# Meta tokens moved behind the tokens in the moving operand of a two-block forward pass

## The chip, the cores and the metric

The kernel runs on one core of one Trainium2 chip. The metric is the device time of one execution in microseconds (us), as the median of the runs. TensorE (PE) does the matmuls, VectorE (DVE) and ScalarE (ACT) prepare operands and take results, GpSimd (POOL) only clears a few constants, and SyncE (SP) issues the weight DMAs.

## The reference

256 tokens of width 2048 pass through two blocks, in float32. The first has an mLSTM branch and a convolution branch, then a feed-forward part; its output is normalised. The second puts 16 meta tokens ahead of the 256 and computes, in short:

```python
h = jnp.concatenate([meta, x], axis=1)            # 16 + 256 rows
u = rmsnorm_2(h, norm1_g)
proj = u @ w_in
v_pool, v_lru, v_gelu, g_pool, g_lru = jnp.split(proj, IN_SPLITS, axis=-1)
pool_out = pool_mixer(v_pool, pool_w, pool_scale)
xc = causal_depthwise_conv(v_lru, conv_w, conv_b)
lru_out = rg_lru(xc, ...) * jax.nn.gelu(v_gelu)
merged = jax.nn.sigmoid(g_pool) * pool_out + jax.nn.sigmoid(g_lru) * lru_out
h = h + merged @ w_out
h = h + jnp.square(jax.nn.relu(rmsnorm_2(h, norm2_g) @ mlp_w1)) @ mlp_w2
out = rmsnorm_2(h, final_g)[:, 16:]
```

Only `v_pool` and `v_lru` are needed for all 272 rows, and so are the gates of the recurrence, which are computed from `xc`. Everything else is needed for the 256 tokens alone.

## The kernel before

**Numbers in two parts.** Each float32 operand is split into a high part (rounded to fp32r) and a low part (the difference). Each product is three matmuls into the same PSUM tile: high weights by high operand, high weights by low operand, low weights by high operand. Weights come in chunks by DMA into `raw`; ACT makes `whi` (line 881) and DVE makes `wlo` (line 1322), half a chunk at a time, three halves ahead of PE (`AHEAD`). There are four slots for each. Weights are the stationary operand; the features stand on the partitions, and the tokens stream.

**Phases and groups.** The program is a list of phases (`plan`), each one weight matrix or a part of it. A group is 4 output tiles of 128 features; with 16 k-tiles it has 192 matmuls of 256 columns (`group`, lines 558 to 560). PE works through two groups' PSUM in turn (`s` is 0 or 1). All engines go through the phases in the same written order. The post-processing of a group (its `step`, in parts j = 0 to 7) is spread over the splits of the group that follows: part j = 0 reads PSUM, and j = 2 of a residual phase sums squares and makes the low operand. The engines wait for each other by semaphores: PE waits for `lo_ready` ahead of every half chunk, for `psum_freed` ahead of every group, and at a phase's first group for the operand (`waits`).

**The normalised operand.** `hn` holds for each k-tile one row of 64 + 2 x 256 floats in each partition, 2304 bytes: 32 unused floats, 16 low and 16 high parts of the meta tokens, 256 high parts, 256 low parts. So the high parts of meta and tokens are one run of 272 floats from float 48 on. The low parts are not one run, and a second tensor `lo2` of 16 rows of 272 floats (1088 bytes) holds them. The gain of the norm is applied in the operand; the scale of each token (one over the root) is applied to the result on its way out of PSUM, with `scale` of 272 floats, whose first 16 are 1.0.

**Wide groups.** `pool_in` and `lru_in` (8 groups) run in `group_wide`, lines 585 to 587, 272 columns: 1536 matmuls. The gates of the recurrence (`gates`, lines 805 to 807) are 192 more, with an operand made in `xc_parts`. `copy_wide` (line 1735) takes the wide results out of PSUM.

**The step that makes the operand of the wide groups.** `down_2` is the last phase of the first block: 4 groups of 11 k-tiles, 132 matmuls each. The DVE step of each group at j = 2 is two sums of squares (line 1350, since two norms are taken together), then `low_operand(..., wide=True)`: four instructions into `hn`, and the same four again into `lo2` (line 1360).

**Halved matmuls.** In some groups one matmul of 256 columns is written as two of 128 (lines 555 and 556): at the last half chunk of a group that has operand waits, and in some phases at an early half chunk. `group_wide` has none.

**Order of tensors in a partition.** `raw`, `whi`, `wlo` and `h` are multiples of 256 bytes each; then comes `gap_a` of 192 bytes, then `hn` (16 x 2304 bytes), then `act` (16 x 2048 bytes). So, counted from the start of `whi` and modulo 256, `hn` and `act` begin at 192.

## Time and profile before

| what | value |
|---|---|
| median of 3 runs | 2707.1 us (2702.05 to 2714.29) |
| the profiled execution, its own time | 2707.32 us |
| its span in the trace | 2705.5 us |
| PE busy in the span | 2669.5 us, 99% |
| DVE busy | 1700.7 us, 63% |
| ACT busy | 1294.6 us, 48% |
| mean granted TensorE clock | 0.996 |

The span goes from the first to the last instruction; the execution's time is 1.8 us more. Matmuls are pipelined: one takes some 277 ns from start to end, and the next starts long before that. So a stretch of PE work is to be read by how many matmuls it starts, which the windows of the trace count, and not by its busy time.

### The profile page before, as it was taken

To read this page: it belongs to the slowest core of one execution; us is meant where nothing else is said; L and a number is where in the kernel's file an instruction comes from. 1 tells how busy PE (TensorE), PEld (TensorE's weight loads), DVE (VectorE), ACT (ScalarE), POOL (GpSimd) and SP (SyncE) were. 2 spreads that over 40 slices of the span, in tenths; PEclk is the share of its full clock that TensorE was granted. 3 is DMA by queue.
4 is the path that set the end of the run, shared out by engine and by line. 5 is a ranking of instruction groups with operands and counts; after the bars stand their busy time and mean duration, and the time that the engine had idled before them with its cause. 6 is when DMAs were issued, how large, how long until landed. Compare 5 with 4: busy or idle time off the path is not lost.

```text
span 2705.5 us, 53096 instructions
## 1 busy us (share of the span) xinstructions
PE 2669.5 (99%) x23022; PEld 2653.9 (98%) x23022; DVE 1700.7 (63%) x1724; ACT 1294.6 (48%) x1459; POOL 1.8 (0%) x14
## 2 busy tenths in 40 slices
PE   8999999999999999999989999999999999999998
PEld 7999999999999999999989999999999999999998
DVE  5665654566776567656785687676666555565565
ACT  6444544445554355435553456664444344343443
POOL 0000000000000000000000000000000000000000
PEclk9999999999999999999999999999999999999999
DMA  6546565555556555565445555555566565555653
GB/s 214 168 159 199 173 202 186 187 195 195 187 186 200 190 192 188 195 198 172 164 168 172 173 176 192 192 188 194 188 194 196 194 191 198 187 192 197 192 194 113
DMA packets 257822, 503.31 MB, mean 186 GB/s; under 512 B 10150, under 2 KB 19038, under 8 KB 257630
## 3 DMA queue, kind: packets, MB, share of 16 engines
q1 hardware_dynamic: 255364, 500.50, 56.1%
q8 instruction: 136, 2.23, 0.3%
q10 hardware_dynamic: 2282, 0.26, 0.1%
q14 instruction: 40, 0.33, 0.0%
HBM read 498.63 MB, written 2.10 MB: 185 GB/s over the span
## 4 chain that ended last, share of the span: by engine, by line
PE 93%; DVE 4%; ACT 2%; issue 1%; DMA 0%; SPq 0%; DVEq 0%; ACTq 0%
PE psum L559 28%; PE psum L558 28%; PE psum L560 28%; PE psum L585 2%; PE psum L586 2%; PE psum L587 2%; DVE wlo L1322 1%; ACT whi L881 1%; DVE work L1350 1%; DVE work L1678 0%; DMA work<-in_x 0%; PE psum L805 0%; PE psum L807 0%; PE psum L806 0%; PE psum L643 0%
## 5 line engine op out<-in xcount | busy, mean ns | idle before, releaser
L1322 DVE TENSOR_TENSOR wlo<-raw,whi 128x1024 fp32r<-128x1024 f32 x952 | 1159.8, 1223 | 923.3 <-ACT whi L881 920.6
L881 ACT ACTIVATE whi<-raw 128x1024 fp32r<-128x1024 f32 x952 | 1004.2, 1059 | 1229.3 <-PE psum L560 1115.6
L559 PE MATMUL psum<-hn,whi 128*128 128x256 f32 x4448 | 1233.3, 277 | 0.0
L558 PE MATMUL psum<-hn,whi 128*128 128x256 f32 x4432 | 1230.6, 278 | 1.8 <-DVE wlo L1322 1.8
L560 PE MATMUL psum<-hn,wlo 128*128 128x256 f32 x4448 | 1232.4, 277 | 0.0
L558 PEld LDWEIGHTS psum<-hn,whi 128*128 128x128 f32 x4432 | 835.5, 189 | 4.6 <-DVE wlo L1322 2.6
L559 PEld LDWEIGHTS psum<-hn,whi 128*128 128x128 f32 x4448 | 836.6, 188 | 0.1
L560 PEld LDWEIGHTS psum<-hn,wlo 128*128 128x128 f32 x4448 | 836.5, 188 | 0.0
L558 PE MATMUL psum<-act,whi 128*128 128x256 f32 x2529 | 700.7, 277 | 14.5 <-DVE wlo L1322 9.7
L559 PE MATMUL psum<-act,whi 128*128 128x256 f32 x2544 | 705.0, 277 | 0.0
L560 PE MATMUL psum<-act,wlo 128*128 128x256 f32 x2544 | 704.1, 277 | 0.0
L558 PEld LDWEIGHTS psum<-act,whi 128*128 128x128 f32 x2529 | 476.3, 188 | 15.6 <-DVE wlo L1322 10.3
L560 PEld LDWEIGHTS psum<-act,wlo 128*128 128x128 f32 x2544 | 479.4, 188 | 0.0
L559 PEld LDWEIGHTS psum<-act,whi 128*128 128x128 f32 x2544 | 479.2, 188 | 0.0
L585 PE MATMUL psum<-hn,whi 128*128 128x272 f32 x512 | 148.8, 291 | 0.0
L586 PE MATMUL psum<-lo,whi 128*128 128x272 f32 x512 | 148.1, 289 | 0.0
L587 PE MATMUL psum<-hn,wlo 128*128 128x272 f32 x512 | 147.4, 288 | 0.0
L585 PEld LDWEIGHTS psum<-hn,whi 128*128 128x128 f32 x512 | 96.9, 189 | 0.0
L587 PEld LDWEIGHTS psum<-hn,wlo 128*128 128x128 f32 x512 | 96.8, 189 | 0.0
L586 PEld LDWEIGHTS psum<-lo,whi 128*128 128x128 f32 x512 | 96.7, 189 | 0.0
L1335 DVE TENSOR_TENSOR work<-psum,scale 128x1024 f32<-128x1024 f32 (+2 forms) x52 | 63.1, 1214 | 22.6 <-PE psum L560 22.6
L1678 DVE SCALAR_TENSOR_TENSOR work<-work,cols 128x256 f32<-128x256 f32 x172 | 71.9, 480 | 1.7
(234 smaller groups left out, 972.8 us busy)
## 6 DMA issues: line engine op xcount, KB each, us to landing
raw<-in_w_in SPq DMA_DIRECT2D x160, 1024.0 KB, 5.1
raw<-in_mlp_w SPq DMA_DIRECT2D x128, 1024.0 KB, 5.2
raw<-in_w_up SPq DMA_DIRECT2D x80, 1024.0 KB, 5.0
raw<-in_w_down SPq DMA_DIRECT2D x40, 1024.0 KB, 5.1
raw<-in_w_out SPq DMA_DIRECT2D x32, 1024.0 KB, 5.1
raw<-in_w_branch_m SPq DMA_DIRECT2D x8, 1024.0 KB, 5.0
raw<-in_w_branch_c SPq DMA_DIRECT2D x8, 1024.0 KB, 5.1
raw<-in_w_up SPq DMA_DIRECT2D x8, 768.0 KB, 4.3
```

Of the source, the lines that this page charges most:

```text
L558: mm(o, hi[:, kk, w], both[:, 0, :], start=first and m % 2 == 0, stop=False)
L559: mm(o, hi[:, kk, w], both[:, 1, :], start=False, stop=False)
L560: last = mm(o, lo[:, kk, w], both[:, 0, :], start=False, stop=end and (m % 2 == 1 or m == tiles - 1))
L585: mm(o, hi[:, kk, w], hn[:, kt, MAIN - META:MAIN + T], start=(kt == 0), stop=False)
L586: mm(o, hi[:, kk, w], lo2[:, kt, :], start=False, stop=False)
L587: last = mm(o, lo[:, kk, w], hn[:, kt, MAIN - META:MAIN + T], start=False, stop=(kt == NT - 1))
L881: A(whi[:, n % SLOTS, :], raw[:, n // 2 % RAW, n % 2 * HALF:(n % 2 + 1) * HALF], ACT.Copy)\
L1322: V.tensor_tensor(wlo[:, n % SLOTS, :], raw[:, n // 2 % RAW, n % 2 * HALF:(n % 2 + 1) * HALF], whi[:, n % SLOTS, :].bitcast(F32), ALU.subt ...
L1335: V.tensor_tensor(dst, summed(ph, i, s, tiles), over_tiles(stream_scale, tiles), ALU.mult)\
L1350: V.tensor_reduce(dst[:, ds(g, 1), :].rearrange("p o t -> p (o t)"), src.rearrange("p k t -> p t k"), AX.X, ALU.add).then_inc(sem("squares ...
L1678: last = V.scalar_tensor_tensor(up_conv[s][:, m, :], up_pad[s][:, m, k:k + T], dcol(f"ffn_w{k}", t), up_conv[s][:, m, :], ALU.mult, ALU.add)
```

## The change

The row of `hn` becomes two halves of 288 floats: 256 high parts, the 16 high parts of the meta tokens, 16 unused; then, 1152 bytes behind, 256 low parts, the 16 low ones, 16 unused. The row has 2304 bytes as before. The wide groups read 272 floats from the start of each half, and the results have the meta tokens in the last 16 columns. `copy_wide` puts them back in front with a copy of their own, and `scale` has only 256 floats. `lo2` and all that wrote it go. `xc_parts` gets the same layout with rows of 2 x 288, and starts at the start of `act`.

```diff
-MAIN = 64
+LOW = 288
...
-        hn = sb("hn", [P, NT, MAIN + 2 * T], F32R)
+        hn = sb("hn", [P, NT, 2 * LOW], F32R)
...
-        meta_lo = hn[:, :, MAIN - 2 * META:MAIN - META]
+        meta_hi, meta_lo = hn[:, :, T:TM], hn[:, :, LOW + T:LOW + TM]
...
-        scale = sb("scale", [P, TM])
+        scale = sb("scale", [P, T])
...
-        with ExitStack() as early:
-            lo2 = sb("lo2", [P, NT, TM], F32R, early)
...
-        xc_parts = [view(act_flat, 16 + j * GW * 2 * TM, GW, 2 * TM) for j in range(2)]
-        lru_pad = [view(heads_flat, at, GW, TM + 3) for at in (0, 2192)]
+        xc_parts = [view(act_flat, j * GW * 2 * LOW, GW, 2 * LOW) for j in range(2)]
+        lru_pad = [view(heads_flat, at, GW, TM + 3) for at in (0, 2304)]
...
-            pool.memset(scale[:, 0:META], 1.0).then_inc(sem("ones_ready"), 1)
...
-                            mm(o, hi[:, kk, w], hn[:, kt, MAIN - META:MAIN + T], start=(kt == 0), stop=False)
-                            mm(o, hi[:, kk, w], lo2[:, kt, :], start=False, stop=False)
-                            last = mm(o, lo[:, kk, w], hn[:, kt, MAIN - META:MAIN + T], start=False, stop=(kt == NT - 1))
+                            mm(o, hi[:, kk, w], hn[:, kt, 0:TM], start=(kt == 0), stop=False)
+                            mm(o, hi[:, kk, w], hn[:, kt, LOW:LOW + TM], start=False, stop=False)
+                            last = mm(o, lo[:, kk, w], hn[:, kt, 0:TM], start=False, stop=(kt == NT - 1))
...
-                return hn[:, kt, MAIN:MAIN + 2 * T].rearrange("p (a t) -> p a t", t=T)
+                return hn[:, kt, :].rearrange("p (a t) -> p a t", t=LOW)[:, :, 0:T]
...
-            run("pool_in", None, waits=[(sem("lo2_made"), 1 + q + 1) for q in range(4)], middle=lambda: norm_total(2, 2),
+            run("pool_in", None, waits=operand_waits(2), middle=lambda: norm_total(2, 2),
...
-            def low_operand(n, g, gain, wide=False):
+            def low_operand(n, g, gain):
...
-                for again in range(2 if wide else 1):
-                    for m in range(GW):
-                        t = GW * g + m
-                        dst = lo2[:, ds(t, 1), META:TM] if again else hn[:, ds(t, 1), MAIN + T:MAIN + 2 * T]
...
+                for m in range(GW):
+                    t = GW * g + m
+                    last = V.scalar_tensor_tensor(hn[:, ds(t, 1), LOW:LOW + T], h[:, ds(t, 1), :], gain(t),
+                                                  hn[:, ds(t, 1), 0:T].bitcast(F32), ALU.mult, ALU.subtract)
+                last.then_inc(sem("operand_split"), 1)
...
-            V.tensor_copy(lo2[:, :, 0:META], meta_lo.bitcast(F32)).then_inc(sem("lo2_made"), 1)
...
-                        V.tensor_tensor(dst(2 * i + s), psum[:, 4 * s:4 * s + 4, 0:TM], over_tiles(scale[:, :]), ALU.mult)\
+                        to, total = dst(2 * i + s), psum[:, 4 * s:4 * s + 4, :]
+                        V.tensor_copy(to[:, :, 0:META], total[:, :, T:TM])
+                        V.tensor_tensor(to[:, :, META:TM], total[:, :, 0:T], over_tiles(stream_scale), ALU.mult)\
                             .then_inc(psum_freed, 1)
```

## Rows read from the trace of the kernel before

**Rows 1.** The page: the chain that ended last, by engine and line.
```profile
PE 93%; DVE 4%; ACT 2%; issue 1%; DMA 0%; SPq 0%; DVEq 0%; ACTq 0%
PE psum L559 28%; PE psum L558 28%; PE psum L560 28%; PE psum L585 2%; PE psum L586 2%; PE psum L587 2%; DVE wlo L1322 1%; ACT whi L881 1%; DVE work L1350 1%; DVE work L1678 0%; DMA work<-in_x 0%; PE psum L805 0%; PE psum L807 0%; PE psum L806 0%; PE psum L643 0%
```

**Rows 2.** PE in windows: start:end, length, busy (matmuls), clock, DMA share, GB/s.
```profile
250.00:300.00 50.00, 50.00 (x444) 1.00 0.58 189
350.00:400.00 50.00, 50.00 (x427) 1.00 0.59 191
1450.00:1500.00 50.00, 50.00 (x399) 1.00 0.52 169
```

**Rows 3.** Groups of instructions, shapes apart: matmuls of both widths.
```profile
L559 PE MATMUL psum<-hn,whi 128*128 128x256 f32 x4448 | 1233.3, 277 | 0.0
...
L559 PE MATMUL psum<-act,whi 128*128 128x256 f32 x2544 | 705.0, 277 | 0.0
...
L586 PE MATMUL psum<-lo,whi 128*128 128x272 f32 x512 | 148.1, 289 | 0.0
...
L806 PE MATMUL psum<-act,whi 128*128 128x272 f32 x64 | 18.4, 288 | 0.0
```

**Rows 4.** Who waited for whom, PE from 1340 to 1395 us: total, times, longest.
```profile
PE psum L558 <- DVE wlo L1322: 9.7, 3, 4.0
```

**Rows 5.** DVE in order of time: start, length, instruction (second, then third stall).
```profile
1364.76 1.23 DVE L1322 TENSOR_TENSOR wlo<-raw,whi 128x1024 fp32r<-128x1024 f32 x1 [4.15 <-ACT whi L881]
1365.90 3.96 DVE L1350 TENSOR_REDUCE work<-work 128x256 f32<-128x1024 f32 x2
1369.78 1.66 DVE L1360 SCALAR_TENSOR_TENSOR hn<-h,gain,hn 128x256 fp32r<-128x256 f32 x4
1371.36 1.66 DVE L1360 SCALAR_TENSOR_TENSOR lo<-h,gain,hn 128x256 fp32r<-128x256 f32 x4
1372.95 4.62 DVE L1322 TENSOR_TENSOR wlo<-raw,whi 128x1024 fp32r<-128x1024 f32 x4
...
1390.60 1.66 DVE L1360 SCALAR_TENSOR_TENSOR lo<-h,gain,hn 128x256 fp32r<-128x256 f32 x4
1392.18 4.61 DVE L1322 TENSOR_TENSOR wlo<-raw,whi 128x1024 fp32r<-128x1024 f32 x4
```

**Rows 6.** All engines in windows: length, PE, PEld, DVE, ACT, POOL, clock, DMA share, GB/s.
```profile
1351.60:1355.30 3.70, 0.49 (x4) 0.31 (x3) 3.70 (x8) 1.06 (x1) 0.00 (x0) 1.00 0.00 0
...
1369.90:1374.40 4.50, 0.53 (x5) 0.33 (x4) 4.50 (x10) 1.06 (x1) 0.00 (x0) 0.95 0.00 0
1374.40:1377.80 3.40, 3.40 (x18) 3.40 (x19) 3.40 (x4) 0.56 (x1) 0.00 (x0) 0.57 0.70 225
...
1390.90:1393.80 2.90, 0.38 (x4) 0.36 (x4) 2.90 (x6) 1.06 (x1) 0.00 (x0) 1.00 0.00 0
...
1394.50:1398.00 3.50, 3.50 (x19) 3.50 (x18) 3.50 (x5) 1.10 (x2) 0.00 (x0) 0.52 0.96 327
...
1412.10:1595.00 182.90, 182.90 (x1454) 182.90 (x1453) 127.23 (x144) 72.63 (x76) 0.00 (x0) 1.00 0.54 179
```

**Rows 7.** PE in order of time, third group of `pool_in`: first matmuls of k-tiles.
```profile
1448.34 0.29 PE L585 MATMUL psum<-hn,whi 128*128 128x272 f32 x1
...
1449.84 0.29 PE L585 MATMUL psum<-hn,whi 128*128 128x272 f32 x1
...
1452.88 0.29 PE L585 MATMUL psum<-hn,whi 128*128 128x272 f32 x1
...
1454.39 0.29 PE L585 MATMUL psum<-hn,whi 128*128 128x272 f32 x1
```

**Rows 8.** DVE instructions by line: duration ns min/median/max, first and last start.
```profile
L1735 DVE TENSOR_TENSOR work<-psum,scale x4: 1291/1292/1292, 1424.3 to 1497.0; 128x1088 f32<-128x1088 f32 x4
...
L1335 DVE TENSOR_TENSOR work<-psum,scale x52: 951/1225/1226, 204.3 to 2602.8; 128x1024 f32<-128x1024 f32 x46, 128x1024 f32 x4, 128x768 f32<-128x768 f32 x2
...
L1390 DVE COPY cols<-psum x1: 174/174/174, 4.0 to 4.0; 128x16 f32<-128x16 f32 x1
```

More of the change, by code:

```diff
@@ L166, in build @@
         r1, r2 = work[:, 8208:8208 + T], work[:, 8464:8464 + T]
-        stream_scale = scale[:, META:TM]
+        stream_scale = scale[:, :]
         def over_tiles(row, n=GW):
@@ L196, in build @@
         act_flat = act[:, :, :].rearrange("p a b -> p (a b)")
-        xc_parts = [view(act_flat, 16 + j * GW * 2 * TM, GW, 2 * TM) for j in range(2)]
-        lru_pad = [view(heads_flat, at, GW, TM + 3) for at in (0, 2192)]
+        xc_parts = [view(act_flat, j * GW * 2 * LOW, GW, 2 * LOW) for j in range(2)]
+        lru_pad = [view(heads_flat, at, GW, TM + 3) for at in (0, 2304)]
         pool_sums = [view(heads_flat, 1100, GW, TM), xc[:, 12:16, :]]
-        gy, gs = view(heads_flat, 4368, GW, T), view(heads_flat, 5392, GW, T)
+        gy, gs = view(heads_flat, 4608, GW, T), view(heads_flat, 5632, GW, T)
         pool_row = (12, 8, 12, 12)
@@ L805, in gates @@
                             mm(o, hi[:, m // 2, k, w], xq[:, kt, 0:TM], start=(k == 0), stop=False)
-                            mm(o, hi[:, m // 2, k, w], xq[:, kt, TM:2 * TM], start=False, stop=False)
+                            mm(o, hi[:, m // 2, k, w], xq[:, kt, LOW:LOW + TM], start=False, stop=False)
                             last = mm(o, lo[:, m // 2, k, w], xq[:, kt, 0:TM], start=False, stop=(k == 1))
@@ L906, in first_high @@
                 for m in range(GW):
-                    last = A(hn[:, GW * q + m, MAIN:MAIN + T], turned(q, m), ACT.Copy, scale=col("norm_mix_g", GW * q + m))
+                    last = A(hn[:, GW * q + m, 0:T], turned(q, m), ACT.Copy, scale=col("norm_mix_g", GW * q + m))
                 last.then_inc(sem("operand_hi"), 1)
@@ L912, in high @@
                 for m in range(GW):
-                    last = A(hn[:, ds(GW * g + m, 1), MAIN:MAIN + T], h[:, ds(GW * g + m, 1), :], ACT.Copy,
+                    last = A(hn[:, ds(GW * g + m, 1), 0:T], h[:, ds(GW * g + m, 1), :], ACT.Copy,
                              scale=gain(GW * g + m))
@@ L940, in meta_root @@
                 ac.wait_ge(sem("meta_loaded"), 16)
-                ac.wait_ge(sem("ones_ready"), 4)
+                ac.wait_ge(sem("ones_ready"), 3)
                 A(meta_sq, meta_nat, ACT.Square, accum_out=meta_ss[:, 0:1]).then_inc(sem("meta_squared"), 1)
@@ L1351, in sum_squares @@
                                 AX.X, ALU.add).then_inc(sem("squares_summed"), 1)
-            def low_operand(n, g, gain, wide=False):
+            def low_operand(n, g, gain):
                 ve.wait_ge(sem("operand_hi"), 4 * n + g + 1)
-                for again in range(2 if wide else 1):
-                    for m in range(GW):
-                        t = GW * g + m
-                        dst = lo2[:, ds(t, 1), META:TM] if again else hn[:, ds(t, 1), MAIN + T:MAIN + 2 * T]
-                        last = V.scalar_tensor_tensor(dst, h[:, ds(t, 1), :], gain(t),
-                                                      hn[:, ds(t, 1), MAIN:MAIN + T].bitcast(F32),
-                                                      ALU.mult, ALU.subtract)
-                    last.then_inc(sem("lo2_made" if again else "operand_split"), 1)
+                for m in range(GW):
[3 more added lines that the diff above has]
+                last.then_inc(sem("operand_split"), 1)
             def scale_from_root(count):
@@ L1377, in first_low @@
                     f = GW * q + m
-                    last = V.scalar_tensor_tensor(hn[:, f, MAIN + T:MAIN + 2 * T], turned(q, m), col("norm_mix_g", f),
-                                                  hn[:, f, MAIN:MAIN + T].bitcast(F32), ALU.mult, ALU.subtract)
+                    last = V.scalar_tensor_tensor(hn[:, f, LOW:LOW + T], turned(q, m), col("norm_mix_g", f),
+                                                  hn[:, f, 0:T].bitcast(F32), ALU.mult, ALU.subtract)
                 last.then_inc(sem("operand_split"), 1)
@@ L1445, in copy_rest @@
                                      cols[:, g1:g1 + NT].unsqueeze(2).to_broadcast([P, NT, META]), ALU.mult))
-                link(V.tensor_copy(hn[:, :, MAIN - META:MAIN], meta_f))
-                link(V.tensor_tensor(meta_lo, meta_f, hn[:, :, MAIN - META:MAIN].bitcast(F32), ALU.subtract))
+                link(V.tensor_copy(meta_hi, meta_f))
+                link(V.tensor_tensor(meta_lo, meta_f, meta_hi.bitcast(F32), ALU.subtract))
             def softplus():
@@ L1657, in step @@
                         else:
-                            low_operand(n, g, gain, double)
+                            low_operand(n, g, gain)
                 return step
@@ L1741, in xc_low @@
                 x = xc_parts[q % 2]
-                low_of(x[:, :, TM:2 * TM], xc[:, 4 * q:4 * q + 4, :], x[:, :, 0:TM], sem("xc_split"))
+                low_of(x[:, :, LOW:LOW + TM], xc[:, 4 * q:4 * q + 4, :], x[:, :, 0:TM], sem("xc_split"))
             into_lru = copy_wide(lambda g: lru_pad[g % 2][:, :, 3:3 + TM])
```

## The prediction

> **What bounds the kernel now.** I read the chain that ended last first: 93% of it is PE, nearly all of that the three matmul lines 558 to 560, and the weight DMAs have no share [rows 1]. So time comes only from PE: from its stalls, from its clock, or from the distance between the starts of two matmuls. Busy time can't show the last of these, so I counted matmuls in windows of 50 us [rows 2]. The reader is to see three paces at the full granted clock (1.00, the 2.4 GHz level). 256 columns start every 50/444 = 112.6 ns from 250 to 300 us, but every 50/427 = 117.1 ns from 350 to 400 us, with the same lines, the same operand and the same addresses. 272 columns start every 50/399 = 125.3 ns; over the whole of the wide phases the count says the same, 1454 in 182.9 us, 125.8 ns [rows 2, 6]. So there is a short and a long pace for one and the same matmul; 16 more columns at 2.4 GHz are 6.7 ns, and the wide matmuls are on neither 112.6 + 6.7 = 119.3 nor 117.1 + 6.7 = 123.8, but above both.
>
> Then I looked for PE's waits in the part that makes the wide operand. In `down_2` PE waits three times for a DVE split, 9.7 us in all [rows 4]. The order of DVE shows why: two sums of squares (3.96 us), four low-operand instructions into `hn`, four into `lo2`, and only then the `wlo` split that PE needs, 1369.78 to 1372.95 for the eight [rows 5]. PE has by then used up the halves made ahead and starts next to nothing from 1369.9 to 1374.4 [rows 6]. After the second and the third of these stalls the granted clock fell: 18 matmuls in 3.4 us at 0.57, 19 in 3.5 us at 0.52, so nearly all at the 1.2 GHz level; after the first (3.7 us window, clock 1.00) it did not [rows 6].
>
> **The change, part by part.**
>
> The second low copy. Four instructions for each of the four groups of `down_2` go. They stand right ahead of the late split, 1371.36 to 1372.95 in one case, 1390.60 to 1392.18 in the other: 1.59 us [rows 5]. Nothing else holds that split (its high half was made while DVE was in the low operand), so each of the three stalls ends 1.59 us sooner, and since each is longer than that, all of it is gained: 3 x 1.59 = 4.8 us. Bounds: 4.8 at the most; at the least 3.2, if one stall finds another cause. The fourth group's copy is made while PE is in `pool_in` and the total of squares; PE is not stalled on it, and it gives nothing. The copy of the meta tokens into `lo2` ahead of the up phase is one DVE instruction under PE work: nothing.
>
> The clock. The stalls become about 1.9, 2.7 and 1.2 us. The shortest after which the clock fell was the third, 2.9 us with its edges. So the third fall should go, and the second is even. Cost of a fall: 18 matmuls at 112.6 ns would take 2.0 of the 3.4 us, so 1.4 lost; 19 (most of them wide, 125 ns) 2.3 of the 3.5, so 1.2 lost. Between nothing and 2.6 I take the middle, 1.3 us.
>
> The pace of the wide matmuls. 1536 of `pool_in` and `lru_in` and 192 of the gates [rows 3] read from new addresses. Counted from `whi` modulo 256 bytes, the high run moves from 128 to 192, the low run from `lo2` (1088-byte rows, so its place moves on by 64 bytes with each k-tile, back after four) to a fixed 64. That the place of an operand has a price is in the trace: of four k-tiles of 12 matmuls the first takes 1449.84 - 1448.34 = 1.50 us, the next two 3.04 together, the fourth 1.51 [rows 7], though nothing differs between them but where they read. What differs with a period of four is the low rows alone. The new low place is not one that I can find in the old wide phases together with the new high one; the 256-column matmuls read high and low at 192, and go at either pace. Bounds: the short pace, 119.3 ns, is 1728 x 6.0 = 10.4 us gained; a loss is bounded by the worst k-tile, 1.52/12 = 126.7 ns, 1728 x 1.4 = 2.4 us. In between lies the long pace without the surplus, 123.8 ns: 1728 x 1.5 = 2.6 us gained. I take this one. The long pace, once there, lasts (50 us without a break in rows 2), some narrow groups have a halved pair of matmuls and the wide ones none, and the wide groups come right after stalls and after the total of squares.
>
> The Trainium skill speaks against any such gain. Its page "SBUF — State Buffer", section "Who interferes with whom", says that PE never waits on any other engine and that its moving operand and its weights have independent read ports. By it the place of an operand is free and this term is nil, a sum of 2701.2 in place of 2698.6. The trace agrees only as far as 1%: the k-tiles differ by that much.
>
> The pace of the narrow matmuls. All 4448 triples on `hn` [rows 3] now find their low rows at 64 instead of 192, with the high rows still at 192. The 2544 triples on `act` are untouched. No row of before has this pair with 256 columns. A gain: if a long-pace stretch such as 350 to 400 us (it lasts some 170 us by the windows between 334 and 501) went to the short pace, 170 x 4.5/117.1 = 6.5 us. A loss: if only the matmul on the low rows took the long pace, 4448 x 4.5 ns = 20 us; if all three did, 60 us. The nearest rows, the wide k-tiles, move by at most 1% with the place of the low rows, and the narrow pace has 112.6 ns with high and low at one place. I take no change, as the pace seems set by what stalled last rather than by the place.
>
> `copy_wide`. One instruction of 1292 ns becomes a copy of 64 elements, 174 ns in the nearest row (16 elements), and one of 1225 ns: 107 ns more, eight times, 0.9 us of DVE [rows 8]. DVE is busy 127 of 183 us there [rows 6], and PE has the other half of PSUM to write meanwhile: nothing. Were DVE the bound there, it would be that 0.9 us. The POOL memset goes, at the start, under the first loads: nothing. The wait of `pool_in` is now for four instructions less of the last group: earlier, so nothing. No DMA is added or moved.
>
> Sum, against the profiled execution (2707.3 us, which is 0.2 above the median of the runs): 2707.3 - 4.8 - 1.3 - 2.6 = 2698.6 us, 0.3% less.
>
> **The rivals.**
>
> *The wide phases take the short pace.* For it: the narrow matmuls do, with high rows at 192, which is where the wide ones now start. Against it: nothing in the wide groups brings the short pace back. 2707.3 - 4.8 - 1.3 - 10.4 = 2690.8 us. 20%.
>
> *The place of the low rows costs the narrow matmuls.* This ends on the other side. Its place is line 559 in all phases on `hn`, its price 4.5 ns on each of 4448 matmuls, 20 us: 2698.6 + 20 = 2719 us; with all three lines 2698.6 + 60 = 2759. It decides from 2 ns per low matmul on (9 us). For it: they are new for 4448 triples, and place matters. Against it: only 1% in the rows that show it. 13%.
>
> *The places do nothing* (the rule above as a mechanism: each matmul's pace is fixed by its columns and by the last stall). 2707.3 - 6.1 = 2701.2 us. 13%.
>
> *The stalls do not shrink as computed:* DVE is freed, but the next split then waits for ACT's high half or a weight chunk. Against it: in the stall DVE runs without a gap and the DMA share is 0.00 [rows 6]. 2707.3 - 2.6 = 2704.7 us or more. 7%.
>
> **How the numbers follow.** The forecast has 47%. Two runs of this kernel differ by up to 0.45%, and 0.5% (13.5 us) is about what a measurement can tell from no change. Faster by more than that means below 2693.6: the short pace (20%) and a part of the forecast, where the second clock fall goes too and a narrow stretch changes pace (6%). Slower means above 2720.6: half of the third case, and the share of paces that come out badly after a stall by chance, 12% together. The rest, 62%, is within. The range reaches from 2685 (short pace, both falls gone, noise) to 2717 (the low rows' price in part), with some 8% below and 12% above. The likeliest case alone spans 2693 to 2704.
>
> **What would show it.** In the profile of the changed kernel: the waits of line 558 for DVE in `down_2` about 4.9 us in place of 9.7; four line-1360 instructions per group; at most one window with the clock near 0.5 after them; 404 wide matmuls in 50 us (123.8 ns), where 399 would mean that the place does nothing and 419 the short pace; 444 or 427 narrow matmuls in 50 us on `hn` as before, and anything between or below means that the low rows' place has a price. The prediction is wrong if the narrow count on `hn` moves, since 13,000 matmuls hang on it.

## The result and the profile after

The changed kernel takes 2751.09 us (median of 4 runs, 2750.86 to 2752.47) and the kernel before 2707.88 us (4 runs, 2702.05 to 2714.29). The ratio is 1.0159, with a 95% interval of 1.0135 to 1.0183: slower by 1.6%, where I had forecast 0.3% faster. Span of the profiled execution: 2750.7 us of 2752.47, mean granted clock 0.996, as before. One execution of a later kernel ("the gain alone") took 2954.01 us at a mean clock of 0.85, and the figures given for that kernel leave it out.

In the chain that ended last PE has 94%. One group of matmuls of the page after:

```profile
L556 PE MATMUL psum<-hn,whi 128*128 128x256 f32 x4448 | 1252.5, 282 | 0.0
```

PE is as much the bound as in [rows 1] (93%), and the count of matmuls is that of [rows 3], but a matmul on `hn` takes 282 ns in the mean where it took 277. PE in windows of 50 us after (columns as in [rows 2]: matmuls in brackets, then clock):

```profile
250.00:300.00 50.00, 50.00 (x427) 1.00 0.56 183
550.00:600.00 50.00, 50.00 (x443) 1.00 0.56 189
1000.00:1050.00 50.00, 50.00 (x427) 1.00 0.56 185
1500.00:1550.00 50.00, 50.00 (x404) 1.00 0.57 186
```

From 250 to 300 us (`hn`) there were 444 matmuls before, now 427: by these counts 117.1 ns instead of 112.6, at a clock of 1.00 both times. From 550 to 600 us PE reads `act`, whose rows did not move: 443, the short pace. The fourth window is the wide phases: 404, so 123.8 ns, where it was 399.

A window also counts the matmuls that it cuts at its edges, about two too many, so the distances worked out from counts (in the prediction too) are some 0.6% too short. `conv_in` has 1152 matmuls; from its first to the first of the next phase it takes 130.56 us before and 135.68 after (next table), which is 113.3 and 117.8 ns. The difference of 4.5 ns is the same either way.

The same work in both kernels, from first matmul to first matmul of the next stretch. Before, all engines (columns as in [rows 6]): `conv_in`, `up_1`, `down_2`, and `pool_in` with `lru_in`:

```profile
182.24:312.80 130.56, 130.56 (x1154) 130.56 (x1153) 71.41 (x63) 63.65 (x75) 0.00 (x0) 1.00 0.60 193
932.55:1106.65 174.10, 174.10 (x1539) 174.10 (x1538) 119.00 (x137) 87.83 (x99) 0.00 (x0) 1.00 0.59 193
...
1317.17:1395.38 78.21, 65.07 (x532) 64.28 (x530) 57.50 (x67) 39.80 (x55) 0.00 (x0) 0.95 0.42 145
1395.38:1593.62 198.24, 198.24 (x1554) 197.83 (x1554) 138.46 (x158) 82.19 (x90) 0.00 (x0) 0.99 0.54 178
```

After, the same four:

```profile
187.58:323.26 135.68, 135.68 (x1155) 135.68 (x1154) 71.31 (x63) 63.59 (x75) 0.00 (x0) 1.00 0.57 186
949.77:1130.69 180.92, 180.92 (x1539) 180.92 (x1538) 119.27 (x137) 88.16 (x99) 0.00 (x0) 1.00 0.58 186
...
1344.63:1418.52 73.89, 65.84 (x532) 65.05 (x530) 52.33 (x55) 39.80 (x55) 0.00 (x0) 0.93 0.44 152
1418.52:1614.60 196.08, 194.88 (x1555) 194.24 (x1554) 137.46 (x161) 81.98 (x90) 0.00 (x0) 1.00 0.55 180
```

The first two grow by 5.12 and 6.82 us with PE busy throughout and the clock at 1.00: 4.4 ns for each matmul, and nobody waits. Four groups on `hn` of the second MLP (from 2341.27 us before, 2379.58 after) grow in the same way, 87.00 to 90.42 us. Summed over all phases in this way, those on `hn` give +49.9 us, those on `act` +1.7, `down_2` -4.3 (78.21 to 73.89), the wide phases and gates -2.3, together +45.0 of the 45.15 us between the two profiled executions. All 13,344 narrow matmuls on `hn` at 4.4 ns would be 59 us; the missing 9 us are matmuls that had no short pace to lose. Most are in `mix_gate` (350 to 400 us in [rows 2]; 1536 matmuls, where the change added only 0.3 us); `up_3`, with three tiles to a group, takes 35.4 us in both kernels, and a part of the first projections was slow before too. Those projections grew by 5.2 us, of which by an estimate 1.7 are not the pace but a stretch at the 1.2 GHz level that comes just ahead of `conv_in` after and not before (first row below: 16 matmuls, where the same window has 33 before).

The clock after, ahead of `conv_in` and at the start of `down_2`:

```profile
177.40:180.80 3.40, 3.40 (x16) 0.51 0.85 266
1358.50:1365.30 6.80, 5.77 (x27) 0.50 0.49 157
```

and at the start of `down_2` before:

```profile
1333.00:1336.40 3.40, 3.40 (x18) 0.50 0.77 299
```

In both kernels this stretch at the lower level stands behind a wait of 3.4 us for `act`, but after it lasted twice as long.

The stalls, PE from 1360 to 1440 us after (total, times, longest):

```profile
PE psum L555 <- DVE wlo L1319: 4.6, 3, 2.4
...
PE psum L525 <- DVE work L1347: 1.2, 1, 1.2
```

and DVE in order of time at the second stall:

```profile
1396.51 1.66 DVE L1355 SCALAR_TENSOR_TENSOR hn<-h,gain,hn 128x256 fp32r<-128x256 f32 x4
1398.09 4.62 DVE L1319 TENSOR_TENSOR wlo<-raw,whi 128x1024 fp32r<-128x1024 f32 x4
```

The split of `wlo` (L1319, L1322 before) starts 1.58 us after the low operand instead of 3.17 [rows 5], and the three waits fell from 9.7 us [rows 4] to 4.6. (They differ somewhat from profile to profile: 9.5, 9.6 and 7.8 us in those of three kernels below that keep the second copy in its place, `wlo` moved by 128 bytes, the halved pair of round 5, everything moved by 64 bytes; 4.5, 5.8 and 6.4 in three that have none.) The second row of waits here is new: the matmul that makes the total of squares (L525) now comes early enough to wait 1.2 us for the sums of the last group. PE behind the second and the third stall after:

```profile
1399.00:1402.50 3.50, 3.14 (x15) 3.15 (x16) 3.50 (x4) 0.14 (x1) 0.00 (x0) 0.56 0.56 159
1417.00:1420.00 3.00, 3.00 (x24) 3.00 (x25) 3.00 (x3) 1.43 (x2) 0.00 (x0) 1.00 0.62 167
```

Behind the second stall the clock still falls (0.56), behind the third no longer (24 matmuls in 3.0 us at 1.00), where [rows 6] had two falls. Together with the longer stretch at the start of `down_2` the clock was at the lower level for about 10.2 us from there to the start of `pool_in`, in both kernels: the third fall is gone and nothing is gained by it.

So the shorter stalls and the wide pace came as meant, the clock gave nothing in sum, and one number spoils it: the pace on `hn`, 427 matmuls in 50 us.

### The profile page after: what moved, and what is told of

Its sections match the earlier page's. It is cut to its first block, busy times and chain, and to the rows that moved or that the text cites. A ratio compares the mean times of both kernels' runs of the same rounds, so it can differ in the third digit from the quotient of the medians.

```text
span 2750.7 us, 53087 instructions
## 1 busy us (share of the span) xinstructions
PE 2720.1 (99%) x23022; PEld 2704.7 (98%) x23022; DVE 1695.8 (62%) x1715; ACT 1295.3 (47%) x1459; POOL 1.7 (0%) x13
## 4 chain that ended last, share of the span: by engine, by line
PE 94%; DVE 3%; ACT 1%; issue 0%; DMA 0%; SPq 0%; DVEq 0%; ACTq 0%
PE psum L556 28%; PE psum L555 28%; PE psum L557 28%; PE psum L584 2%; PE psum L583 2%; PE psum L582 2%; DVE wlo L1319 1%; DVE work L1347 1%; ACT whi L878 1%; DMA work<-in_x 0%; DVE work L1671 0%; PE psum L802 0%; PE psum L525 0%; PE psum L804 0%; PE psum L640 0%
## 5 line engine op out<-in xcount | busy, mean ns | idle before, releaser
L1319 DVE TENSOR_TENSOR wlo<-raw,whi 128x1024 fp32r<-128x1024 f32 x952 | 1161.2, 1223 | 967.4 <-ACT whi L878 965.1
L556 PE MATMUL psum<-hn,whi 128*128 128x256 f32 x4448 | 1252.5, 282 | 0.0
L555 PE MATMUL psum<-hn,whi 128*128 128x256 f32 x4432 | 1247.4, 281 | 1.0 <-DVE wlo L1319 0.9
L557 PE MATMUL psum<-hn,wlo 128*128 128x256 f32 x4448 | 1246.9, 280 | 0.0
L556 PEld LDWEIGHTS psum<-hn,whi 128*128 128x128 f32 x4448 | 838.2, 188 | 0.1
L555 PEld LDWEIGHTS psum<-hn,whi 128*128 128x128 f32 x4432 | 834.5, 188 | 3.4 <-issue 1.7
L555 PE MATMUL psum<-act,whi 128*128 128x256 f32 x2529 | 701.9, 278 | 8.7 <-DVE wlo L1319 4.6
L556 PE MATMUL psum<-act,whi 128*128 128x256 f32 x2544 | 706.1, 278 | 0.0
L555 PEld LDWEIGHTS psum<-act,whi 128*128 128x128 f32 x2529 | 476.6, 188 | 9.9 <-DVE wlo L1319 5.2
L556 PEld LDWEIGHTS psum<-act,whi 128*128 128x128 f32 x2544 | 480.6, 189 | 0.0
L582 PE MATMUL psum<-hn,whi 128*128 128x272 f32 x512 | 146.5, 286 | 0.0
L583 PE MATMUL psum<-hn,whi 128*128 128x272 f32 x512 | 146.3, 286 | 0.0
L583 PEld LDWEIGHTS psum<-hn,whi 128*128 128x128 f32 x512 | 96.8, 189 | 0.0
L582 PEld LDWEIGHTS psum<-hn,whi 128*128 128x128 f32 x512 | 96.8, 189 | 0.0
```

What stands on the lines that cost most here:

```text
L555: mm(o, hi[:, kk, w], both[:, 0, :], start=first and m % 2 == 0, stop=False)
L556: mm(o, hi[:, kk, w], both[:, 1, :], start=False, stop=False)
L557: last = mm(o, lo[:, kk, w], both[:, 0, :], start=False, stop=end and (m % 2 == 1 or m == tiles - 1))
L582: mm(o, hi[:, kk, w], hn[:, kt, 0:TM], start=(kt == 0), stop=False)
L583: mm(o, hi[:, kk, w], hn[:, kt, LOW:LOW + TM], start=False, stop=False)
L1319: V.tensor_tensor(wlo[:, n % SLOTS, :], raw[:, n // 2 % RAW, n % 2 * HALF:(n % 2 + 1) * HALF], whi[:, n % SLOTS, :].bitcast(F32), ALU.subt ...
```

## The experiments

Below, the *place* of a row is its first byte counted from the start of `whi`, modulo 256. Before, all token rows of `hn` and `act`, high and low, are at 192 (rows of 2304 and 2048 bytes keep it for every k-tile), with the low row 1024 bytes behind the high one in both. After, `hn` is at 192 (high) and 64 (low). Counts are matmuls of 256 columns in 50 us at a clock of 1.00; 443 or 444 is the short pace. The diffs are excerpts. Where one time stands without a range it is a single execution; those of the kernel before lie between 2699.48 and 2714.29 us in all rounds, so such a time shows a loss of 40 us and no small one.

### Round 1: is it the distance, the place, or the waits?

**One part alone.** The kernel before, with nothing changed but where the rows of `hn` lie (the high one at 64, the low one 1152 bytes behind it at 192).

```diff
-MAIN = 64
+MAIN = 32
+LOWER = MAIN + 288
...
-        hn = sb("hn", [P, NT, MAIN + 2 * T], F32R)
+        hn = sb("hn", [P, NT, 576], F32R)
...
```

> The kernel before with one part of the change alone: low rows 1152 bytes behind the high ones (high rows start 128 bytes earlier in the row to make room). lo2, the wide operand and the scale stay as before. Places are counted from the start of whi, modulo 256 bytes: high 64, low 192, act 192 and 192. Difference theory (the short pace needs high and low rows that start at the same place modulo 256): all matmuls on hn take the long pace, 427 in 50 us, those on act stay at 443 or 444, the kernel takes some 2707 + 52 = 2755 to 2765 us. Wait theory (the changed kernel is long-paced because it stalls at other moments and nothing brings it back): most phases on hn keep 444, 2700 to 2715 us.

Measured: 2751.25 us, beside 2703.54 for the kernel before. PE in windows:

```profile
250.00:300.00 50.00, 50.00 (x426) 1.00 0.55 183
550.00:600.00 50.00, 50.00 (x443) 1.00 0.55 189
```

The whole loss is there with every other part of the change left out. `copy_wide`, the waits, the meta tokens and `lo2` have no share in it.

**High and low at one place.** The kernel after, with the low rows in a region of their own, 18432 bytes (72 x 256) behind the high ones. With rows of 1152 bytes both are at 192 in even k-tiles and both at 64 in odd ones.

```diff
-        hn = sb("hn", [P, NT, 2 * LOW], F32R)
+        hn = sb("hn", [P, 2 * NT, LOW], F32R)
...
-                            mm(o, hi[:, kk, w], hn[:, kt, LOW:LOW + TM], start=False, stop=False)
+                            mm(o, hi[:, kk, w], hn[:, NT + kt, 0:TM], start=False, stop=False)
...
```

> The changed kernel with all high rows first and all low rows behind them, 1152 bytes for each row: low 18432 bytes behind high, so both at the same place modulo 256, which is 192 for even k-tiles and 64 for odd ones. All else as in the changed kernel. Difference theory: hn phases at 444 in 50 us, and the kernel at 2750 - 50 = 2695 to 2703 us, faster than before. Place theory (a row that starts at 64 is what costs, whatever its partner): odd k-tiles of hn are long, about 435 in 50 us or all long, 2725 to 2752 us.

Measured: 2730.36 us (2721.96 to 2731.77), ratio 1.0085 (1.0060 to 1.0109).

```profile
250.00:300.00 50.00, 50.00 (x427) 1.00 0.56 188
550.00:600.00 50.00, 50.00 (x444) 1.00 0.56 190
1000.00:1050.00 50.00, 50.00 (x434) 1.00 0.55 189
```

Half of the loss is back, but the first window is as long as ever: that high and low are at one place is not enough. The third window, in `up_1`, lies between the two paces because k-tiles differ there. An even and then an odd k-tile of 12 matmuls, from first matmul to first matmul:

```profile
989.49:990.86 1.37, 1.37 (x14) 1.00 0.96 374
990.86:992.27 1.41, 1.41 (x14) 1.00 0.01 3
```

Over all of `up_1` the even ones (place 192) have 113.9 ns and the odd ones (64) 117.8. So here the pace goes by the place of the k-tile being read, and the short one is back at the next k-tile; in `conv_in` (the first window) even and odd ones are long alike, 117.5 and 118.1 ns.

**All rows moved by 128 bytes.** The kernel after with `gap_a` 16 floats instead of 48 ahead of `hn`: `hn` at 64 and 192, and `act` at 64.

```diff
-        sb("gap_a", [P, 48])
+        sb("gap_a", [P, 16])
```

> The changed kernel with gap_a of 64 instead of 192 bytes, so hn and act lie 128 bytes nearer to the weights: high 64, low 192, act 64 and 64. Difference theory: as the changed kernel, hn 427 and act 443 in 50 us, 2745 to 2756 us. Place theory: act is now at 64 and goes long too (2544 triples, up to 33 us more), 2770 to 2785 us, with hn long or half of it short.

Measured: 2766.52 us.

```profile
250.00:300.00 50.00, 50.00 (x427) 1.00 0.55 182
550.00:600.00 50.00, 50.00 (x427) 1.00 0.51 174
2300.00:2350.00 50.00, 50.00 (x437) 1.00 0.58 190
```

Now `act` (550 to 600 us) is long too, though its two rows are 1024 bytes apart as ever. So it is the place and not the distance. The third window, a later phase on `act` with the same rows, shows that place 64 is not long without exception: 437 lies between.

**Low rows 1088 bytes behind.** The kernel after with low rows at 0.

```diff
-LOW = 288
+LOW = 272
+ROW = 576
...
```

> The changed kernel with low rows 1088 bytes behind the high ones in the same 2304-byte rows: high 192, low 0. 1088 bytes is where a row of 272 ends, so in the wide groups the low row starts where the high one ends. Difference theory: narrow matmuls on hn long (427 or fewer in 50 us), no gain over the changed kernel. End-to-start theory (the short pace needs a row to start, modulo 256, where the last one ended): narrow long, but the wide groups get faster than the 404 in 50 us of the changed kernel. Place theory (64 costs): hn short again, near 2700 us.

Measured: 2763.68 us.

```profile
250.00:300.00 50.00, 50.00 (x422) 1.00 0.54 180
```

422 is 118.5 ns by the count: place 0 for the low row is worse than 64.

### Round 2: a map of places, and the second copy removed with the rows left where they were

Three kernels change only gaps or the low rows' offset. The first two are the kernel before with `hn` at 0 and `act` at 128, and with `hn` at 64 and `act` at 0; the third is the kernel after with its low rows 1216 bytes behind, at 128.

```diff
-        sb("gap_a", [P, 48])
+        sb("gap_a", [P, 16])
         hn = sb("hn", [P, NT, MAIN + 2 * T], F32R)
+        sb("gap_b", [P, 48])
```

(this is the second; the first has no `gap_a` and a `gap_b` of 32, the third `LOW = 304` in rows of 576 floats).

> The kernel before with other gaps ahead of hn and act, the rows themselves as before (low rows 1024 bytes behind high ones, so both at one place). Places from whi modulo 256: hn 0 and 0, act 128 and 128, where before had 192 and 192 for both. Difference theory (same place is enough): all phases keep 443 or 444 in 50 us, 2700 to 2712 us. Window theory (the short pace needs high and low rows both at 192, which the first four experiments leave open): hn and act both at 427 or fewer, 2707 + 85 = 2790 us or more.

> As the last one, with hn at 64 and 64 and act at 0 and 0. The run with everything moved by 128 bytes had act at 64 and 64, and most of its act phases were long. Difference theory: 443 or 444 everywhere. Window theory: hn as act was there, 427, and act at 0 long as well, 2785 us or more.

> The changed kernel with low rows 1216 bytes behind the high ones: high 192, low 128, act 192 and 192. Difference theory and window theory both say long on hn (427 or fewer in 50 us; 1152 and 1088 gave 427 and 422), 2750 to 2765 us. If it is short, what counts is neither, but that 64 and 0 are bad places for low rows.

Measured: 2816.87, 2795.81 and 2761.61 us, beside 2707.41 before. In the first, `hn` at 0, then `act` at 128:

```profile
250.00:300.00 50.00, 50.00 (x419) 1.00 0.54 181
550.00:600.00 50.00, 50.00 (x424) 1.00 0.53 180
```

In the second, `hn` at 64, then `act` at 0:

```profile
250.00:300.00 50.00, 50.00 (x427) 1.00 0.56 189
550.00:600.00 50.00, 50.00 (x419) 1.00 0.54 175
```

In the third, `hn` at 192 and 128:

```profile
250.00:300.00 50.00, 50.00 (x424) 1.00 0.54 179
```

The pace follows the place, in `hn` and `act` alike: 0 gives 419 in both. A high row at 192 with the low one elsewhere (427, 424 and 422 for 64, 128 and 0) goes about as if both were elsewhere.

**The gain alone.** The kernel before without `lo2`, token rows still at 192: the meta tokens' low parts lie behind the low row, in the unused floats ahead of the next one, the low matmul writes PSUM from column 16 on, split in two (256 and 16 columns) in the first k-tile, and DVE adds the last 16 columns to the first.

```diff
...
-                            mm(o, hi[:, kk, w], lo2[:, kt, :], start=False, stop=False)
+                            low = hn_low[:, kt, MAIN + T - META:MAIN + 2 * T]
+                            if kt == 0:
+                                mm(psum[:, 4 * s + m, META:TM], hi[:, kk, w], low[:, 0:T], start=False, stop=False)
+                                mm(psum[:, 4 * s + m, TM:TM + META], hi[:, kk, w], low[:, T:TM], start=False, stop=False)
+                            else:
+                                mm(psum[:, 4 * s + m, META:META + TM], hi[:, kk, w], low, start=False, stop=False)
...
```

> The gain of the change without its price: no lo2 and four DVE instructions fewer per group of down_2, but high and low rows stay 1024 bytes apart, both at 192. The meta tokens' high parts stand ahead of the high rows and their low parts behind the low rows (in the unused floats of the next row), the low matmul of a wide group writes 16 columns further right in PSUM, and a small DVE add joins the meta columns; at the first k-tile it is two matmuls (32 more in all). act comes ahead of hn so that both keep their place. Both theories: narrow phases on hn at 443 or 444, down_2 5 us shorter than before, the wide phases at 124 to 126 ns, 2695 to 2703 us, faster than before by 0.2 to 0.4%.

Measured: 2707.66 us (median of 9, 2698.85 to 2712.65, four of them from 2711.5 up), beside 2707.41; ratio 1.0005 (0.9987 to 1.0022). The waits in `down_2`:

```profile
PE psum L559 <- DVE wlo L1328: 6.4, 3, 2.4
PE psum L529 <- DVE work L1356: 0.7, 1, 0.7
```

and PE in three windows (`conv_in`, `mix_gate`, wide):

```profile
200.00:250.00 50.00, 50.00 (x444) 1.00 0.60 201
400.00:450.00 50.00, 50.00 (x427) 1.00 0.55 183
1450.00:1500.00 50.00, 50.00 (x402) 1.00 0.53 175
```

With the rows at 192 the short pace is back and the 45 us are gone, though the second copy is still out. In the profile `down_2` was 4.6 us shorter and the wide phases 2.6 us longer (1.35 and 1.23 us; they hold the added small matmuls), which leaves 2 us of gain, less than the medians can tell. No profile exists of the executions at 2711.5 to 2712.7 us.

### Round 3: relative or absolute, how narrow, and the two paces at one place

**Everything moved by 64 bytes**, and **`hn` at 160 with `act` at 224**, both from the kernel before.

```diff
+        sb("gap_0", [P, 16])
         raw = sb("raw", [P, RAW, CK * NC])
```

```diff
-        sb("gap_a", [P, 48])
+        sb("gap_a", [P, 40])
         hn = sb("hn", [P, NT, MAIN + 2 * T], F32R)
+        sb("gap_b", [P, 16])
```

> The kernel before with 64 unused bytes ahead of all its tensors: every address moves by 64 bytes, and no place relative to whi changes. Relative theory (the distance from operand to weights modulo 256 sets the pace): 443 or 444 in 50 us as before, 2700 to 2712 us. Absolute theory (the operand's own address counts): hn and act behave as hn did at place 0, about 120 ns, 2800 us or more.

> The kernel before with hn at place 160 and act at place 224 (from whi, modulo 256), high and low 1024 bytes apart: 32 bytes to each side of the 192 that is short. Measured so far for 256 columns: 192 short, 113.4 ns; 64 mostly long, 117.8; 128 118.7; 0 120.0. If the window around 192 is wide, both stay short, 2700 to 2715 us; if it is 192 alone, both are long, 2790 us or more; one side alone open gives 50 (hn long) or 25 us (act long) more than before.

Measured: 2701.98 and 2792.14 us, beside 2702.11 before. The first, `conv_in` and `mix_gate`:

```profile
250.00:300.00 50.00, 50.00 (x443) 1.00 0.59 190
400.00:450.00 50.00, 50.00 (x443) 1.00 0.59 192
```

The second, `hn` at 160, then `act` at 224:

```profile
250.00:300.00 50.00, 50.00 (x424) 1.00 0.56 181
550.00:600.00 50.00, 50.00 (x425) 1.00 0.55 182
```

A shift of all these tensors does nothing, so what counts is a place relative to something that moved along. And 32 bytes to either side of 192 cost the full price.

**The second copy later**, in part j = 4 of the residual step instead of j = 2; and the same **with one matmul cut in halves (a halved pair) in half chunk 1 of every group**, the wide ones too.

```diff
-                            low_operand(n, g, gain, double)
+                            low_operand(n, g, gain)
+                    elif j == 4 and double:
+                        low_operand(n, g, gain, (1,))
...
```

```diff
-                            if k == halved and kk == 0 and m == 0:
+                            if k in (halved, 1) and kk == 0 and m == 0:
...
```

> The kernel before with one edit: the four instructions into lo2 are made two halves later (part j = 4 of the residual step instead of j = 2), so that the late wlo split comes ahead of them. The layout stays. Stall theory: the three stalls shrink by 1.6 us each as in the changed kernel, of which 1.2 us come back as a wait for the sum of squares in pool_in, and one clock fall goes: 2707 - 4.8 + 1.2 - 1.3 = 2702 us, on average 0.1 to 0.2% faster than before. If the deferred copies only move the stall, no change.

> The last kernel with a halved matmul (two of 128 columns, or two of 136 in the wide groups) at the second half chunk of every group. If a halved pair brings back the short pace where high and low rows are both at 192: mix_gate at 113.4 instead of 117.2 ns in every execution, 6 us less, and the spread between executions (2701 to 2708) narrower; 2694 to 2698 us. In the wide groups the short pace would be 120 ns, 9 us less again; if their rows at 128 and in lo2 don't allow it, they stay at 125 to 126.

Measured: 2703.95 us (12 runs, 2700.04 to 2711.15), ratio 1.0004 (0.9991 to 1.0018); and 2714.98 us (7 runs, 2711.78 to 2716.52), ratio 1.0040 (1.0027 to 1.0054), both beside 2702.11. The waits in `down_2` of the first:

```profile
PE psum L558 <- DVE wlo L1322: 7.4, 3, 3.4
PE psum L528 <- DVE work L1350: 2.5, 1, 2.5
```

The stall only moved, to the sums of squares. In the second, `mix_gate` and a wide stretch:

```profile
400.00:450.00 50.00, 50.00 (x444) 1.00 0.58 189
1450.00:1500.00 50.00, 50.00 (x400) 1.00 0.54 180
```

`mix_gate` is short. That is no proof for the halved pair: it is as short without one in the profile of the kernel just above (443 from 400 to 450 us), in the shifted one (443) and in the one with `wlo` moved (round 4, 444). The wide phases stay at 125 ns by the count: a halved pair does nothing for them. The pairs cost about 0.12 us for each of the 108 groups that got one, which is the 12.9 us over the kernel before.

### Round 4: whose matmul is slow, and whose address counts

**Another order.** In the first kernel, made from the one after, the matmuls of a k-tile are put in two runs, 8 on the high row and then 4 on the low one; the second is the same edit to the kernel before, as a control.

```diff
-                            mm(o, hi[:, kk, w], both[:, 1, :], start=False, stop=False)
-                            last = mm(o, lo[:, kk, w], both[:, 0, :], start=False,
+                            mm(o, lo[:, kk, w], both[:, 0, :], start=False, stop=False)
+                        for m in range(tiles):
+                            o = psum[:, 4 * s + m // 2, m % 2 * T:(m % 2 + 1) * T]
+                            last = mm(o, hi[:, kk, m * P:(m + 1) * P], both[:, 1, :], start=False,
...
```

> The changed kernel with the narrow matmuls of each k-tile in another order: for the four output tiles high weights and low weights by the high row (8 matmuls), then high weights by the low row (4). The same matmuls, but PE goes from one row to the other twice in 12 instead of eight times. Transition theory (a step from a row at 192 to one at 64 costs, and not the row itself): most triples regain 113.4 ns, hn phases near 440 in 50 us, 2705 to 2720 us. State theory (as soon as any row stands off 192, the short pace is lost for all matmuls around it): 427 as before, 2750 us. Own-row theory (each matmul is paced by its own row): the 8 at 192 take 113.4 and the 4 at 64 take more, 433 or so in 50 us, 2725 to 2735 us.

> The kernel before with the same new order, all rows at 192: the control for the last one. Nothing should change, 443 or 444 in 50 us and 2700 to 2713 us; if the order itself costs, it shows here.

Measured: 2751.47 us, ratio 1.0185 (1.0168 to 1.0202), and 2714.09 us, beside 2701.64 before. `conv_in` of the first, and one of its k-tiles in order of time (L555 and L556 read the high row, L559 the low one; some rows left out):

```profile
250.00:300.00 50.00, 50.00 (x427) 1.00 0.58 189
```

```profile
230.28 0.28 PE L555 MATMUL psum<-hn,whi 128*128 128x256 f32 x1
...
231.22 0.64 PE L559 MATMUL psum<-hn,whi 128*128 128x256 f32 x4
231.69 0.28 PE L555 MATMUL psum<-hn,whi 128*128 128x256 f32 x1
```

The control, `conv_in`, `mix_gate` and `up_1`:

```profile
200.00:250.00 50.00, 50.00 (x427) 1.00 0.57 188
400.00:450.00 50.00, 50.00 (x427) 1.00 0.57 184
1000.00:1050.00 50.00, 50.00 (x444) 1.00 0.62 204
```

If only matmuls on the low row were slow, or only the changes from one row to the other, fewer changes or a third of the matmuls would have shown: a third slow is 438 in 50 us. It is 427 in either order, and the rows show it directly: the 8 matmuls on the high row, which is at 192, take 0.94 us, 117.5 ns each, and the 4 on the low row 0.47 us, the same. So one row off its place takes the short pace from all matmuls of its k-tile. The control shows the other side: with all rows at 192 a phase can still be long (`conv_in` and `mix_gate` here), as `mix_gate` is in [rows 2]. It is one execution, and its 2714.09 us are within what the kernel before reaches by itself; whether the order had a part in the long `conv_in` is open, but the order alone does not make a phase long, since `up_1` is short in it.

**`wlo` moved by 128 bytes**, `hn` and `act` kept where they were.

```diff
         whi = sb("whi", [P, SLOTS, HALF], F32R)
+        sb("gap_w", [P, 32])
         wlo = sb("wlo", [P, SLOTS, HALF], F32R)
...
-        sb("gap_a", [P, 48])
+        sb("gap_a", [P, 16])
```

> The kernel before with 128 unused bytes between whi and wlo and 128 fewer behind h: hn and act keep their addresses, so they stay at 192 from whi, but are at 64 from wlo. If the pace comes from the distance between the operand and the weights loaded meanwhile, both kinds of weights count: the short pace is lost for all or for a part of each triple, 2720 to 2800 us. If only whi counted, or only the operand's address in steps of 256 from some fixed point that moves with the first tensor, 2700 to 2712 us.

Measured: 2700.78 us.

```profile
250.00:300.00 50.00, 50.00 (x444) 1.00 0.58 189
```

The place of the low weights, and of `h` that moved with them, made no difference here.

### Round 5: the gain with `mix_gate` made short

The kernel of "the gain alone" and the kernel before, both with a halved pair in half chunk 1 of every other group of `mix_gate` (those with s = 0).

```diff
-                            if k == halved and kk == 0 and m == 0:
+                            if k == (1 if ph.name == "mix_gate" and s == 0 else halved) and kk == 0 and m == 0:
```

> The kernel with the split meta tokens (f4: no lo2, both rows at 192) and one more edit: in mix_gate the first matmul of the second half chunk is halved in every other group. State theory: a pace lost by a stall at the start of mix_gate comes back at the next halved pair, so mix_gate takes 175 to 176 us in every execution instead of 174.6 or 180.6, and the kernel 2697 to 2701 us, faster than before by 0.1 to 0.2%. If the halved pair does nothing here, the executions spread from 2699 to 2712 as f4's did.

> The kernel before with the halved matmul in mix_gate alone. State theory: no execution above some 2704 us, 2701 to 2702 us in all, while the kernel before itself varies between 2701 and 2714. Without effect: the same spread as before.

Measured: 2699.72 us (11 runs, 2698.77 to 2706.32), ratio 0.9996 (0.9986 to 1.0006); and 2702.10 us (11 runs, 2700.87 to 2708.82), ratio 1.0004 (0.9995 to 1.0013), both beside 2701.18 (21 runs, 2699.48 to 2713.31). `mix_gate` was short in both profiles (443 matmuls from 400 to 450 us).

Neither can be told from the kernel before. The executions of that kernel lie mostly near 2701 or near 2707.5, and `mix_gate` on the long pace is worth 6 us (180.57 us for 174.61), the distance between the two; that this is what parts them was seen in profiles of kernels near to it and not shown for its own executions. One execution of the last kernel was at 2708.8 all the same, and in this round 19 of 21 executions of the kernel before were near 2701 without any halved pair.

## Why the prediction was wrong

The step that failed is the pace of the narrow matmuls on `hn`: "I take no change, as the pace seems set by what stalled last rather than by the place". I put it at nothing; it was +49.9 us, nearly all of it pace (`conv_in`: 113.3 to 117.8 ns). I had the bound right (a loss of 60 us "if all three did") and the sign at stake named as a rival, but gave it 13% and sized it at 20 us, as if only the matmul on the low rows could slow. The measured case is the 2759 us version of that rival, less some 10 us that had no short pace to lose, plus 2 us each for the act phases and for what the clock and the new wait took from the gains. That the measured time comes near this version is no credit to the forecast, which had all three lines slow only as a bound. Two inferences misled me. [Rows 2] show two paces at one and the same place, and I took that as proof that place has no part; the runs show that both hold: place 192 is needed for the short pace, and a phase can lose it even there. And I took the 1% between wide k-tiles [rows 7] as the size of the effect, though the wide matmuls never had the short pace to lose (399 to 404 in 50 us in the windows shown, so 123.8 ns at best by the count).

The other steps, one by one:

- *The stalls.* Right: 9.7 us to 4.6, so 5.1 for the forecast 4.8, by the mechanism given (four instructions less ahead of the split; the profiles of like kernels spread by 1 to 2 us around either figure). What I left out is what is late next: the total of squares, 1.2 us of new wait.
- *The clock.* Wrong in its gain of 1.3 us. One fall less behind the stalls, the third, as forecast, but the stretch at the 1.2 GHz level at the start of `down_2` lasted 6.8 us for 3.4, so the sum is the same 10.2 us in both, and there is one more stretch at 177.4 us. Nor do like stalls bring like falls: the reordered kernel of round 4, with 5.8 us of such stalls, had the lower level for 3.4 us in `down_2`, and the one with `wlo` moved, with 9.5 us, for 13.6 us up to `pool_in`. One profile of each kernel can't price this term.
- *`down_2` as a whole* is 4.3 us shorter. PE's idle time there fell by 5.1 (78.21 - 65.07 to 73.89 - 65.84) and its busy time rose by 0.8. The longer stretch at half the clock accounts for about that: PE was busy in it for 5.77 us instead of 3.40 (1.2 us of work lost), against half a microsecond saved where the third fall had begun.
- *The wide pace.* Right in size: 404 in 50 us, as forecast; `lru_in` went from 96.85 to 95.57 us, 1.7 ns for each of 768 matmuls where I had 1.5. `pool_in` with `lru_in` gained 2.2 us on balance: 198.24 to 196.08, that is 1.2 of new wait against 1.2 for the clock fall that is gone and 2.2 for the pace.
- *`copy_wide`.* Right that it costs nothing: the wide phases have no wait for it. The copy of 64 elements took 225 ns for the 174 that I had taken.
- *The act phases.* +1.7 us in sum, nearly all in `out2` and the first `mlp2` phase (0.75 each), though their rows did not move; forecast nothing, and the cause is open.

By what the stalls and the wide pace gave alone the sum would have been near 2700 us. No run measured that. The kernel of "the gain alone" shows that `down_2` keeps its gain (4.6 us) with the rows at 192, but it pays 2.6 us in the wide phases, and its median cannot be told from that of the kernel before.

Against the wide gain I had weighed the Trainium skill, page "SBUF — State Buffer", section "Who interferes with whom": PE waits for no other engine, and moving operand and weights have independent read ports. From this I concluded that every place is equal; the section itself says nothing of an operand's address. The conclusion does not hold here: the same program with `hn` at 0 and `act` at 128 takes 2816.87 us for 2707.41. Whether the ports are independent no run here shows.

Left open: why a row's place matters at all, and against what it is counted. Moving all tensors changes nothing and moving `wlo` and `h` changes nothing, so it is `whi`, `raw` or something placed behind `hn`; I took `whi` as the origin without showing that it is. A conflict between reading the moving operand and loading the weights is my guess, and only that; the run with `wlo` moved gives it no support, since a third of the matmuls have their weights from there. What other engines and the DMAs write meanwhile was varied by no run. Also open: what makes a phase with all rows in place come out long; a halved pair early in the group went with the short pace in the three profiles that have one in `mix_gate`, but so did three of the six without, and `conv_in`, which has none in eight of these nine kernels, was short in seven of those eight.

## What to carry to other kernels

A tensor's offset is a parameter to be measured: when an edit changes a row's length or start, keep the address of what PE streams (here modulo 256 bytes) or measure the pace again, above all for the operand that most matmuls read. Busy time hides this, so count matmuls in windows of equal length before and after, at equal clock. And multiply each uncertain price by its count before giving it a chance: 4.4 ns on some 11,000 of the 13,344 matmuls outweighed every stall in the forecast.

## What the runs showed of the hardware that I had not expected

- PE's distance between starts for 256 columns depends on the place of the moving operand. By counts in 50 us it is 112.6 ns with high and low rows at 192, 117.6 to 117.9 at 160, 224 and 128, 117.1 at 64 (not in every phase), 119.3 at 0. From first matmul to first matmul of whole phases (`conv_in` for places of `hn`, `out1` for places of `act`) the same are 113.3, 118.3 to 118.7, 117.8 and 120.0 ns. Between best and worst of these kernels lie 116 us.
- One row of two off its place slows the matmuls on both, in either order tried (all 12 of a k-tile near 117.5 ns). It need not last: with even k-tiles at 192 and odd ones at 64, `up_1` had 113.9 and 117.8 ns by turns, while `conv_in` was long throughout.
- Where all rows are in place there are still two paces, and which one a phase takes differs from profile to profile (`mix_gate`: 427 or 443 in 50 us), with the granted clock at 1.00 in both.
- Cutting one matmul in halves costs about 0.12 us for its pair.
